# A depthwise convolution's taps moved onto one engine in a two-block transformer kernel

## What is computed

```python
def second_block(x, ...):
    for l in range(DEPTH):                       # 2 layers
        x = x + 0.5 * swiglu_ffn_2(...)
        u = rms_norm(x, mix_norm[l]) @ w_in[l]
        y_conv = conformer_conv(u_conv, ...)     # below
        y_pool = multiscale_pool(u_pool, ...)
        o = diff_attention(q, k, v, lam, slopes)
        y = jnp.concatenate([y_conv, y_pool, y_attn], axis=-1) @ w_out[l]
        x = x + y
        x = x + 0.5 * swiglu_ffn_2(...)

def conformer_conv(u, w_dw, b_dw, ln_g, ln_b):
    a, gate = jnp.split(u, 2, axis=-1)           # 256 channels each
    z = a * jax.nn.sigmoid(gate)
    z = lax.conv_general_dilated(z, w_dw[:, None, :], ..., # width 31, one filter for each channel
        feature_group_count=D_CONV) + b_dw
    return jax.nn.silu(layer_norm(z, ln_g, ln_b))
```

## Time and profile before

| | |
|---|---|
| median of 3 runs | 2071.75 us (2071.15 to 2075.09) |
| profiled execution, its span | 2071.1 us |
| PE busy | 2049.5 us, 99% |
| DVE busy | 1501.6 us, 73% |
| ACT busy | 1095.9 us, 53% |
| POOL busy | 129.0 us, 6% |

### The profile page before, as it was taken

One profiled execution on the slowest core, in us unless ns is written; L12 is line 12 of the kernel. 1 busy time (PEld: TensorE's weight loads), 2 busy tenths in 40 slices (PEclk: granted clock), 3 DMA queues, 4 the chain that ended last, 5 costly groups with the idle time before them and its releaser, 6 DMA issues.

```text
span 2071.1 us, 27842 instructions
## 1 busy us (share of the span) xinstructions
PE 2049.5 (99%) x10800; PEld 1750.2 (85%) x10800; DVE 1501.6 (73%) x2261; ACT 1095.9 (53%) x1637; POOL 129.0 (6%) x140
## 2 busy tenths in 40 slices
PE   9999999999999999999999999999999999999998
PEld 8888888888888888888888888878888888878887
DVE  6776677777677766777776777798667777797766
ACT  5444664544554456655446554675444544675443
POOL 1000100000000001000000000160000000160000
PEclk9999999999999999999999999999999999999999
DMA  8654545555555555455565755535555655535553
GB/s 253 200 187 166 188 152 192 187 186 188 186 191 183 193 165 172 154 197 193 184 192 181 246 185 193 171 103 195 194 194 185 200 190 183 173 113 193 191 193 125
DMA packets 105539, 378.82 MB, mean 183 GB/s; under 512 B 12173, under 2 KB 12837, under 8 KB 105152
## 3 DMA queue, kind: packets, MB, share of 16 engines
q1 hardware_dynamic: 102768, 368.95, 54.0%
q0 software_dynamic: 2208, 7.71, 1.3%
q10 hardware_dynamic: 432, 0.39, 0.1%
HBM read 375.73 MB, written 1.27 MB: 182 GB/s over the span
## 4 chain that ended last, share of the span: by engine, by line
PE 93%; DVE 4%; ACT 1%; DMA 0%; issue 0%; POOL 0%; POOLq 0%; DVEq 0%; ACTq 0%
PE pb L429 31%; PE pb L434 16%; PE pb L357 13%; PE pb L358 13%; PE pb L359 13%; DVE scr L1703 2%; PE pb L382 1%; DVE wlo L1689 1%; PE pb L480 1%; PE pb L404 1%; PE pb L403 1%; PE pb L402 1%; DVE scr L2360 0%; PE pb L541 0%; DVE X L1703 0%; DMA raw<-in_W 0%
## 5 line engine op out<-in xcount | busy, mean ns | idle before, releaser
L1689 DVE TENSOR_TENSOR wlo<-raw,whi 128x1024 fp32r<-128x1024 f32 (+1 forms) x702 | 849.1, 1217 | 54.3 <-ACT whi L1072 53.8
L1072 ACT ACTIVATE whi<-raw 128x1024 fp32r<-128x1024 f32 (+1 forms) x706 | 730.6, 1045 | 294.0 <-PE pb L434 164.7
L429 PE MATMUL pb<-XT,whi 128*128 128x512 f32 x2816 | 705.0, 392 | 3.5 <-DVE XT L1703 2.7
L429 PEld LDWEIGHTS pb<-XT,whi 128*128 128x128 f32 x2816 | 515.6, 189 | 104.9 <-DVE XT L1703 4.3
L434 PEld LDWEIGHTS pb<-XT,wlo 128*128 128x128 f32 x2816 | 384.3, 191 | 27.5
L434 PE MATMUL pb<-XT,wlo 128*128 128x256 f32 x2816 | 392.8, 283 | 0.0
L1798 DVE TENSOR_REDUCE sbuf_s<-pb 128x256 f32<-128x512 f32 x240 | 154.6, 686 | 234.8 <-PE pb L434 234.8
L357 PE MATMUL pb<-whi,HTh 128*128 128x512 f32 x816 | 322.0, 395 | 1.0 <-DVE HTl L1703 1.0
L358 PE MATMUL pb<-wlo,HTh 128*128 128x512 f32 x816 | 320.2, 392 | 0.0
L359 PE MATMUL pb<-whi,HTl 128*128 128x512 f32 x816 | 318.3, 390 | 0.0
L1142 ACT ACTIVATE sbuf_s<-sbuf_s 128x256 f32<-128x256 f32 x120 | 49.6, 419 | 342.5 <-DVE sbuf_s L1805 342.4
(11 more groups left out here) (231 smaller groups left out, 1493.6 us busy)
## 6 DMA issues: line engine op xcount, KB each, us to landing
raw<-in_W SPq DMA_DIRECT2D x694, 512.0 KB, 4.2
raw<-in_W SPq DMA_DIRECT2D x8, 264.0 KB, 2.8
scr<-in_bc POOLq DMA_DIRECT2D x2, 640.0 KB, 5.9
raw<-in_W SPq DMA_DIRECT2D x4, 256.0 KB, 4.6
scr<-scratch POOLq DMA_DIRECT2D x8, 128.0 KB, 4.0
scr<-mrow POOLq DMA_DIRECT2D x2, 512.0 KB, 5.0
scr<-in_slope POOLq DMA_DIRECT2D x1, 1024.0 KB, 11.1
scr<-in_Pg POOLq DMA_DIRECT2D x1, 1024.0 KB, 14.3
```

Of the source, the lines that this page charges most:

```text
L429: pe.matmul(pb[b + j][:, :], h[:, k:k + P], xs, start=c == 0, stop=False)
L1072: return act.activation(o, i, ACT.Copy, scale=scale)
L1689: dve.tensor_tensor(wlo[u % W_SLOTS][:, 0:c], raw[u % RAW_SLOTS][:, 0:c], whi[u % W_SLOTS][:, 0:c].bitcast(F32), ALU.subtract).then_inc(*u ...
```

## The change

All 31 taps of both channel halves are made by DVE. Where DVE had one instruction for tap j it now has two, for half 0 and half 1, in the same place of its list; each waits for its own half's tap j - 1, so that neighbours do not wait for each other. ACT's 31 taps, POOL's 30 adds, the eight slots and the waits between them go. `turn_conv` waits for one signal instead of two. The order of everything else is as before.

```diff
                 def turn_conv(b):
-                    w.wait_ge(*at("tap_v", i, 30))
-                    w.wait_ge(*at("tap_p", i, 30))
+                    w.wait_ge(*at("tap_v", i, 30, 1))
...
-                def tap(j):
-
-                    s1, w1 = zp[:, 1, j:j + S], cw[:, 31 + j:32 + j]
-                    w.wait_ge(*at("zp", i))
-                    w.wait_ge(*at("cw", i))
-                    if j == 0:
-                        act.activation(acc[:, 1, :], s1, ACT.Identity, scale=w1, bias=cw[:, 63:64]).then_inc(
-                            *up("tap_a", i, j))
-                    else:
-                        if j > TAP_SLOTS:
-                            w.wait_ge(*at("tap_p", i, j - TAP_SLOTS))
-                        copy(taps[:, j % TAP_SLOTS, :], s1, w1).then_inc(*up("tap_a", i, j))
...
                 def tap(j):
 
-                    s0, w0 = zp[:, 0, j:j + S], cw[:, j:j + 1]
                     if j == 0:
                         w.wait_ge(*at("zp", i))
                         w.wait_ge(*at("cw", i))
-                        dve.tensor_scalar(acc[:, 0, :], s0, w0, cw[:, 62:63], ALU.mult, ALU.add).then_inc(
-                            *up("tap_v", i, j))
-                    else:
-                        w.wait_ge(*at("tap_v", i, j - 1))
-                        axpy(acc[:, 0, :], s0, w0, acc[:, 0, :], ALU.mult, ALU.add).then_inc(*up("tap_v", i, j))
+                    for c in range(2):
+                        o, s0, w0 = acc[:, c, :], zp[:, c, j:j + S], cw[:, 31 * c + j:31 * c + j + 1]
+                        if j == 0:
+                            dve.tensor_scalar(o, s0, w0, cw[:, 62 + c:63 + c], ALU.mult, ALU.add).then_inc(
+                                *up("tap_v", i, j, c))
+                        else:
+                            w.wait_ge(*at("tap_v", i, j - 1, c))
+                            axpy(o, s0, w0, o, ALU.mult, ALU.add).then_inc(*up("tap_v", i, j, c))
...
-                def add_tap(j):
-                    w.wait_ge(*at("tap_a", i, 0))
-                    w.wait_ge(*at("tap_a", i, j))
-                    done = one("tap_p", i, j)
-                    pool.tensor_tensor(acc[:, 1, :], acc[:, 1, :], taps[:, j % TAP_SLOTS, :], ALU.add).then_inc(*done)
```

More of the change, by code:

```diff
@@ L42 @@
 WARM_UP = (8, 5)
-TAP_SLOTS = 8
 def spans(items):
@@ L255, in program @@
         aT = two(part2("aT"))
-        taps = part2("tap").rearrange("p (i t) -> p i t", i=TAP_SLOTS)
         columns, used_columns = {}, [0] * 4
@@ L1549, in mixer2 @@
                 conv_in(4)
[L1550 to L1553, removed]
                 split(u0 + 6 + AHEAD)
                 split(u0 + 7 + AHEAD)
-                tap(4)
-                tap(7)
                 split(u0 + 8 + AHEAD)
-                tap(5)
-                tap(6)
                 squares("q", 0, 7, 2)
                 squares("q", 1, 7, 2)
-                tap(12)
                 lam_exp()
[L1565 to L1568, removed]
                 split(u0 + 9 + AHEAD)
-                tap(14)
                 split(u0 + 11 + AHEAD)
                 split(u0 + 10 + AHEAD)
-                tap(13)
                 squares("k", 0, 11, 0)
@@ L1576, in mixer2 @@
                 split(u0 + 12 + AHEAD)
-                tap(16)
-                tap(10)
                 turned("q", qT2, gq, 0, 5)
                 split(u0 + 14 + AHEAD)
-                tap(17)
                 turned("q", qT2, gq, 1, 6)
@@ L1586, in mixer2 @@
                 split(u0 + 15 + AHEAD)
-                tap(18)
                 turned("k", kT2, gk, 0, 7)
                 turned("k", kT2, gk, 1, 4)
[L1590 to L1595, removed]
                 exp(0, 5)
@@ L1598, in mixer2 @@
                 exp(0, 6)
-                tap(26)
-                tap(25)
                 pool_high(1, 7)
@@ L1604, in mixer2 @@
                 exp(0, 2)
-                tap(29)
                 exp(0, 0)
                 exp(0, 3)
-                tap(27)
                 pool_high(0, 7)
                 exp(1, 6)
-                tap(28)
                 exp(1, 7)
                 exp(1, 0)
-                tap(30)
                 exp(1, 4)
@@ L2737, in mixer2 @@
                 norm_root(n)
[L2738 to L2744, removed]
                 head_root("q")
-                add_tap(8)
-                add_tap(9)
                 head_root("k")
[L2749 to L2769, removed]
                 conv_root()
```

## The result

| | before | after |
|---|---|---|
| time, same chip | 2071.75 us (2071.15 to 2075.09) | 2079.97 us (2078.46 to 2080.38) |
| profiled execution, its span | 2071.1 us | 2077.9 us |
| the time of that execution | not recorded | 2079.76 us |
| forecast | | 2077.3 us (2073.0 to 2081.0) |

The changed kernel is slower: ratio 1.0034, 95% interval 1.0022 to 1.0045. On a second chip, in a later run, it was 2079.87 us against 2072.46, ratio 1.0036 (1.0023 to 1.0050). Of the seven runs of after, one took 3421.40 us at a mean granted clock of 0.555, where the others had 0.998 or 0.999; the range and the ratio leave it out. The result lies in the forecast's range, 2.7 us above the forecast itself; most of this document is about those 2.7.

A forecast was written before the change was run, and what follows sets the result against it. PE, busy 99%, sets the end, with DVE behind its waits in the changed stretches. Mixers 1.1 (with -1.65 for the clock) and 2.35, plus 2.1 for new falls: +5.6, span 2076.7, median 2077.3 us (2073.0 to 2081.0).

The forecast's parts named there:

- Taps and their pitch: DVE's taps ahead of `head_out("k")`: an alternating pair costs 0.80 us, so taps 0 to 7 take 6.4.
- What PE's path gives back: Between `job(14, 0)` and the first `biased`: PE's path needs 4.1 us, giving back 0.6 in the first mixer, 1.4 in the second.
- part 1: First mixer, taps ahead of `head_out("k")`: DVE gets there 4.1 us later, and `job(14, 0)` starts 4.1 late.
- the two terms -0.4 and -0.85: First mixer, before the maps' transposes: `maps_max` shortens by 0.4 us, DVE's remaining list up to `difference(0, 2)` by 0.85.
- The sum without the clock: Delay from added DVE work, no clock effect: 2.75 us in the first mixer, 2.35 in the second.
- The clock: Half clock behind `job(14, 0)` costs 1.05 us in each mixer; the first mixer's old fall behind the maps goes, -1.65.
- From span to time: Whole kernel: the median time stands 0.65 us above the profiled span, so 2076.7 becomes 2077.3.
- The gain of 1.65 from the lost fall: First mixer, behind the maps' wait: the shorter wait of 1.5 us keeps the clock, winning back 1.65 us.
- A: DVE's taps: alternation does not help, each still costs 0.52 us behind its neighbour; 2088 us, chance 0.06.
- B: DVE's taps: each costs less than 0.40 us without POOL's traffic, so not slower; 2068.4 us, chance 0.07.
- C: PE at `job(14, 0)`: the clock holds through the new wait; 2075.2 us, chance 0.20.
- D: ACT's split ahead of `turned("k")` waits for a late load, holding the maps in both mixers; 2080 to 2081 us, chance 0.09.

The follow-up runs named there:

- filler12_again: Changed kernel with 12 filler products on PE ahead of `job(14, 0)`, inside PE's wait, rerun on one chip with the unaltered changed kernel: 2076.56 us.
- before_fill7: Kernel before with seven filler products on PE ahead of the first maps' transposes, inside PE's wait: 2071.68 us, ratio 0.9996.
- serial: Changed kernel without the alternation: in each group of neighbouring taps, all of half 0's stand ahead of half 1's: 2088.99 us, ratio 1.0081.
- early_taps: Kernel before with the second half's taps 0 to 21 moved to DVE, 22 to 30 left on ACT and POOL: 2077.35 us, ratio 1.0020.
- late_taps: Kernel before with only the second half's taps 22 to 30 moved to DVE, 0 to 21 left on ACT and POOL: 2077.05 us, ratio 1.0014.
- kfirst2: Changed kernel with both `head_out` of k and `up_low` placed ahead of taps 18 to 21 in DVE's list: 2080.14 us, ratio 1.0033.
- after_again: Changed kernel unaltered, rerun on one chip beside its version with 12 filler products: 2079.87 us.

## Why the prediction was right, and why it was 2.7 us short

**Taps and their pitch: right.** A pair costs 0.80, as in the earlier trace rows. Taps 0 to 7 took 6.21 instead of 6.4, mostly since the two instructions of tap 0 stand 0.33 apart. From tap 0 to `job(14, 0)` it is now 1361.67 - 1332.56 = 29.11, before 25.32: +3.8 against +4.1 forecast. PE's three waits were 0.95, 2.85 and 1.37 us, forecast 1.3, some 3.2 and 1.5.

**What PE's path gives back: mis-sized.** The prediction let the first `biased` follow 4.1 behind `job(14, 0)`, 3.34 to the logits and 0.8 on to the first maps. The logits were right: 1362.11 to 1365.46 in filler12_again. But the first `biased` came 1.33 behind them (timeline of DVE, filler12_again):

```profile
1366.79 0.42 DVE L2318 CUSTOM_DVE_ANT_0 scr<-pb,scr 128x256 f32<-128x256 f32 x1 [0.54 <-PE pb L870]
```

Before it had been 1362.65 - 1361.28 = 1.37, so the row was there to be read. 4.7 and not 4.1: nothing is given back in the first mixer instead of 0.6. In the second mixer it came 1836.12 - 1831.56 = 4.56 behind the job, so 0.95 was given back and not 1.4. The errors, -0.3 in part 1 and +0.6 or +0.45 here, partly cancel, and the rest holds: from `maps_max` to the maps' transposes it was 1381.39 - 1365.61 = 15.78 and is 1385.44 - 1370.94 = 14.50, -1.3, where the two terms -0.4 and -0.85 stood.

**The sum without the clock: right, with some luck.** 2.73 and 2.48 us (filler12_again against before_fill7), forecast 2.75 and 2.35.

**The clock: right in kind and place, mis-sized.** Half clock behind `job(14, 0)` in both mixers, none behind the maps. But a fall took 1.4 to 1.74 us, not 1.05. The prediction let part of the slow stretch fall into the wait; none did, since the 3.4 us of half clock began only at about 1362.3, when `job(14, 0)` (1361.67) was already running. The prediction's bounds for it, 0 to 1.6, held nearly all. In after's profile the logits follow `job(14, 0)` by 1366.63 - 1361.67 = 4.96 instead of 3.35, and DVE stood 1.86 for the pooling's product and 0.53 for the logits. Net, -1.5 and twice 1.5 to 1.65 make +1.5 to +1.8 where the forecast had -1.65 + 2.1 = +0.45: about **1.2 us** of the 2.7.

**From span to time: wrong.** The prediction set the median 0.65 above the span. In every execution here where both are known it lies between 1.76 and 2.13, nearly always under 1.95: 2079.76 and 2077.9, 2076.86 and 2075.0, 2071.61 and 2069.8. By that offset the profiled execution of before, with 2071.1, belongs to a run of about 2073.0, one with a fall; the median was 2071.75. The gain of 1.65 from the lost fall was counted against an execution that was slower than the median, and the small offset of 0.65 hid this. That is the other **1.2 us**. The rest, 0.3, lies in the 0.1 of the clock-free sum and in the profiled execution of after, 0.2 below its median. What is won back of a disturbance that only some executions have must not be taken from the median.

**The rivals.** A (2088) fell with the pairs at 0.80, and its price was too low: serial, with 30 of A's 46 chained steps, already took 2088.99. B fell with the 0.40 of each tap. C (the clock holds, 2075.2) did not happen of itself but was made by hand: 2076.56 to 2076.98, 1.4 to 1.8 above, of which 1.2 is the offset again. D fell, as what ACT stood for just ahead of `turned` was PE and not a load (timeline of ACT, after):

```profile
1364.94 0.69 ACT L1069 ACTIVATE scr<-pb,hcol 128x512 f32<-128x512 f32 x1 [2.87 <-PE pb L478]
```

A load some 7 us ahead had been late for ACT, but the split was done before DVE and PE asked for it.

The rule on a free-running gate (the Trainium skill, TensorE: Matmul & The Clock Gate, Part 1) that the prediction weighed agrees with early_taps and late_taps, each with one length of wait in two mixers and two outcomes; that the gate runs freely is not shown by it. The 424 ns that the Trainium skill's formula (VectorE: DVE Perf Modes, the TRN2 errata section) gives for an op of 256 columns do not agree as a distance, as the starts lie 0.40 apart. Nor does what the prediction drew from the Trainium skill's "The DRAIN you can't avoid" (VectorE: DVE Perf Modes), that a dependent op costs no more: 0.52 against 0.40.

## What to carry to other kernels

Moving work from idle engines to the one that releases the matmuls pays only if the contention it removes is larger than the instructions it adds; here 7.7 us against 12.9 with no fall of the clock in either, 8.6 against 16.0 with the falls, though the whole-kernel share of that engine was 73%. Price a wait of TensorE with the stretch of half clock that may follow it, here 1.4 to 1.74 us behind waits of 2 to 3 us, and test for it by filling the wait with products that nobody reads. Before a term "won back" goes into a sum, find out whether the execution that you subtract from is the median one, by the offset between span and time.

## What the hardware showed that was not expected

- Half clock follows a wait with no fixed rule that these runs would show: it fell behind gaps of 2.24 us, 2.82 and 2.93, and held behind others of 2.82 and 2.94. Behind one of 3.55 (kfirst2) it lasted 6.8 us, behind one of 3.61 (serial, second mixer) 3.4, as elsewhere.
- 2.8 us of meaningless products in the wait make a kernel 3.3 us faster and narrow its runs from 2.7 us (after_again) to 0.9 (filler12_again).
- Chained taps cost 0.52 us from start to start with nothing else running, alternating ones 0.40, and the two `tensor_scalar` of tap 0 0.33.
- Adds of POOL slowed seven chained taps from 3.60 to 5.26 us.
